# Layers written out, clearing moved to idle GpSimd, loads carried over layer ends, and one block for each stage's addition, norm, turning and first products

## The reference

```python
for l in range(2):                                   # first block
    proj = rms_norm(x, attn_norm[l]) @ w_in[l]       # 1024 x 3328
    mix = three mixers of proj (attention, differential attention, gated scan)
    x = x + mix @ w_out[l]
    hf = rms_norm(x, ffn_norm[l]) @ w_up[l]          # gate and value, 2816 each
    x = x + (gelu(conv(gate)) * value) @ w_down[l]
for l in range(2):                                   # second block
    proj = x @ w_in_2[l]
    mix = rms_norm by head of four mixers of proj    # short conv, MLA, conformer conv, windowed attention
    h = layer_norm(ALPHA * x + mix @ w_out_2[l], ln1_g, ln1_b)
    # 8 heads, each choosing 16 of 16384 experts; computed as a dense product over all of them
    x = layer_norm(ALPHA * h + peer_ffn(h), ln2_g, ln2_b)
```

## Time and profile before

| | |
|---|---|
| runs | 3116.73 us median of 3 (3116.24 to 3126.63) |
| profiled execution | 3117.86 us, of which the span from first to last instruction is 3116.1 |
| busy, share of the span | PE 2696.1 us (87%), VectorE 2165.6 (69%), ScalarE 1465.3 (47%), GpSimd 351.3 (11%) |
| mean granted TensorE clock | 0.909 |
| HBM traffic | 161 GB/s over the span |

### The profile page before, as it was taken

The page is one execution under the profiler, slowest core; times in us unless marked ns, Lnnn a source line. Parts: engine busy times, 40 slices in busy tenths (PEclk is TensorE's granted clock), DMA queues, the critical chain, the costliest instruction groups (busy, mean ns, idle before and its releaser), DMA issues. The chain is left out here.

```text
span 3116.1 us, 57779 instructions
## 1 busy us (share of the span) xinstructions
PE 2696.1 (87%) x16968; PEld 2432.3 (78%) x16968; DVE 2165.6 (69%) x4756; ACT 1465.3 (47%) x2850; POOL 351.3 (11%) x308
## 2 busy tenths in 40 slices
PE   7858978768968579989999999675799899999996
PEld 6657967558966479979997888564799799978885
DVE  5766757656756755887777777557558877767775
ACT  5334545335433334546665555332345456655553
POOL 3130003130002003430000000030024300000000
PEclk9858999769988589999999999885899999999998
DMA  5104545014534045655556777440456555567774
GB/s 189 58 34 142 184 137 181 27 54 154 183 139 138 9 143 178 228 169 175 175 171 230 240 242 240 144 171 1 142 174 229 172 174 173 172 228 239 241 243 146
DMA packets 193620, 504.00 MB, mean 162 GB/s; under 512 B 22496, under 2 KB 88288, under 8 KB 191968
## 3 DMA queue, kind: packets, MB, share of 16 engines
q1 hardware_dynamic: 193504, 502.62, 48.2%
HBM read 467.93 MB, written 34.60 MB: 161 GB/s over the span
## 5 line engine op out<-in xcount | busy, mean ns | idle before, releaser
L165 DVE TENSOR_TENSOR w_lo<-w_raw,w_hi 128x512 fp32r<-128x512 f32 x1376 | 938.5, 686 | 337.1 <-ACT w_hi L156 307.3
L156 ACT ACTIVATE w_hi<-w_raw 128x512 fp32r<-128x512 f32 (+1 forms) x1592 | 925.0, 621 | 301.6 <-PE ffn_up L198 95.9
L196 PE MATMUL up_up<-hT_hi,w_hi 128*128 128x256 f32 x2048 | 596.2, 291 | 26.6 <-DVE w_lo L165 20.5
L197 PE MATMUL up_up<-hT_lo,w_hi 128*128 128x256 f32 x2048 | 582.2, 284 | 0.0
L198 PE MATMUL up_up<-hT_hi,w_lo 128*128 128x256 f32 x2048 | 582.1, 284 | 0.0
L174 POOL TENSOR_TENSOR w_lo<-w_raw,w_hi 128x512 fp32r<-128x512 f32 (+2 forms) x216 | 292.7, 1355 | 1999.4 <-DVE w_lo L165 1981.5
L196 PEld LDWEIGHTS up_up<-hT_hi,w_hi 128*128 128x128 f32 x2048 | 395.3, 193 | 31.0 <-DVE w_lo L165 23.8
L208 PE MATMUL peer_acc<-w_hi,expert_hi 128*128 128x512 f32 x1024 | 400.1, 391 | 7.8 <-DVE w_lo L165 7.8
L209 PE MATMUL peer_acc<-w_lo,expert_hi 128*128 128x512 f32 x1024 | 399.4, 390 | 0.0
L210 PE MATMUL peer_acc<-w_hi,expert_lo 128*128 128x512 f32 x1024 | 399.3, 390 | 0.0
L197 PEld LDWEIGHTS up_up<-hT_lo,w_hi 128*128 128x128 f32 x2048 | 395.9, 193 | 0.0
(11 more groups left out here) (367 smaller groups left out, 4579.8 us busy)
## 6 DMA issues: line engine op xcount, KB each, us to landing
w_raw<-in_peer_u_c SPq DMA_DIRECT2D x256, 512.0 KB, 3.3
w_raw<-in_peer_v SPq DMA_DIRECT2D x256, 512.0 KB, 3.3
w_raw<-in_w_up_c SPq DMA_DIRECT2D x88, 512.0 KB, 3.3
expert_gelu_held<-expert_gelu SPq DMA_DIRECT2D x256, 128.0 KB, 1.7
expert_back<-expert_gelu_held SPq DMA_DIRECT2D x256, 128.0 KB, 3.0
w_raw<-in_w_down SPq DMA_DIRECT2D x44, 512.0 KB, 3.8
w_raw<-in_w_in_r SPq DMA_DIRECT2D x40, 512.0 KB, 3.4
w_raw<-in_w_in_c SPq DMA_DIRECT2D x32, 512.0 KB, 4.4
```

What stands on the lines that cost most here:

```text
L156: self.nc.scalar.activation(self.w_hi[:, k % SLOTS, 0:width], self.raw_half(k, width), ACT.Copy).then_inc(self.sem("w_hi_done"), 1)
L165: self.nc.vector.tensor_tensor(self.w_lo[:, k % SLOTS, 0:width], self.raw_half(k, width), self.w_hi[:, k % SLOTS, 0:width].bitcast(F32), A ...
L196: self.nc.tensor.matmul(bank, hi, self.hT_hi[:, c, :], start=(c == 0), stop=False)
L197: self.nc.tensor.matmul(bank, hi, self.hT_lo[:, c, :], start=False, stop=False)
```

## The change

- The two loops over layers are written out in Python, with constants for l. `new_scope` makes new semaphores for each part of a layer; the old ones are cleared by `sweep` on GpSimd, within the block of the next feed-forward loop or of `up_with_gates`. The weight stream's own semaphores and counters run on through the program.
- The last stage of a layer (`gated_loop`, `DownPhase`) loads the first four pieces of the next one (`after`). Columns of all layers and the rotary table are loaded and made in the first block.
- `transpose_split`, `rms_rows` and, for `ln1` and the first `ln2`, `layer_norm` become entries (`TurnEntry`, `RmsEntry`, `LayerNormEntry`), whose steps stand at the head of the lists of `project` or `gated_loop`, in the same block as the first products, and with them the addition, which reads PSUM. PSUM is held as two sets of four banks, left and right, from stage to stage. The products of a chunk wait for that pair of chunks alone. The norm's factor isn't applied to the rows but to the identity (`diag`), and the turning is a real product with it. The first four halves (`EARLY`) are split inside the entry, all `w_lo` on VectorE. For a layer norm, x itself is finished by `rows`, one of four passes after each weight half from the ninth.
- `head_norm` and `layer_norm` take eps and the mean in ScalarE's Sqrt (scale and bias) and drop one VectorE operation; the mixers' gain of the second kind goes into the copies that evict the turned chunks.
- The last layer norm and the store are `finish`: by token halves, rows loaded in free weight slots beside the last products; GpSimd clears what is left during the store.

```diff
+    def new_scope(self):
+        self.stale += list(self.sems.values())
+        self.sems = {}
+    def sweep(self, pool):
+        for s in self.stale:
+            pool.sem_clear(s)
+            self.nc.release_semaphore(s)
+        self.stale = []
...
+            if entry is not None:
+                entry.chunk_ready(pe, c)
...
+    def chunk_ready(self, pe, c):
+        if c % 2 == 0:
+            pe.wait_ge(self.lo_done, c // 2 + 1)
+    def tensor(self, pe):
+        for t in range(TT):
+            if self.add is not None:
+                pe.wait_ge(self.added, t + 1)
             for c in range(DC):
-                for t in range(TT):
-                    ins = nc.tensor.transpose(ps[:, c, t * P:(t + 1) * P],
-                                              src[:, t, c * P:(c + 1) * P], K.ident[:])
-                ins.then_inc(turned, 1)
-
-        @block.scalar
-        def _(act):
+                ins = self.K.nc.tensor.transpose(self.ps[:, c, t * P:(t + 1) * P], self.src[:, t, c * P:(c + 1) * P],
+                                                 self.K.ident[:])
+                if t == TT - 1 and c % 2 == 1:
+                    ins.then_inc(self.turned, 1)
+    def scalar(self, act):
+        for h in range(EARLY):
+            self.K.split_hi(act, self.k0 + h)
+        self.evict_hi(act)
+    def evict_hi(self, act):
+        A, hi = self.K.nc.scalar, self.K.hT_hi
+        for j in range(DC // 2):
+            act.wait_ge(self.turned, j + 1)
+            if self.gain is None:
+                ins = A.activation(hi[:, 2 * j:2 * j + 2, :], self.ps[:, 2 * j:2 * j + 2, :], ACT.Copy)
+            else:
+                for c in (2 * j, 2 * j + 1):
+                    ins = A.activation(hi[:, c, :], self.ps[:, c, :], ACT.Copy, scale=self.gain[:, c:c + 1])
+            ins.then_inc(self.hi_done, 1)
...
+    def vector(self, dve):
+        for t in range(TT):
+            if self.add is not None:
+                x = self.src[:, t].rearrange("p (h n) -> p h n", h=2)
+                self.K.nc.vector.tensor_tensor(x, x, self.add[:, t], ALU.add).then_inc(self.added, 1)
+        for h in range(EARLY):
+            self.K.split_lo(dve, self.k0 + h)
+        self.evict_lo(dve)
...
+class RmsEntry(TurnEntry):
...
+    def tensor(self, pe):
+        for t in range(TT):
+            pe.wait_ge(self.scaled, t + 1)
             for c in range(DC):
-                act.wait_ge(turned, c + 1)
-                g = 1.0 if gain is None else gain[:, c:c + 1]
-                nc.scalar.activation(K.hT_hi[:, c, :], ps[:, c, 0:SEQ], ACT.Copy,
-                                     scale=g).then_inc(hi_done, 1)
-
-        @block.vector
-        def _(dve):
+                ins = self.K.nc.tensor.matmul(self.ps[:, c, t * P:(t + 1) * P], self.src[:, t, c * P:(c + 1) * P],
+                                              self.diag[:, t, :], start=True, stop=True)
+                if t == TT - 1 and c % 2 == 1:
+                    ins.then_inc(self.turned, 1)
+    def scalar(self, act):
+        A = self.K.nc.scalar
+        for h in range(2):
+            self.K.split_hi(act, self.k0 + h)
+        for t in range(TT):
+            if self.add is not None:
+                act.wait_ge(self.added, t + 1)
+            A.activation(self.junk[:, t, :], self.src[:, t, :], ACT.Square,
+                         accum_out=self.ss[:, t, 0:1]).then_inc(self.squared, 1)
+            act.wait_ge(self.squared, t + 1)
+            A.activation(self.ss[:, t, 1:2], self.ss[:, t, 0:1], ACT.Sqrt, scale=1.0 / D,
+                         bias=self.K.eps[:, 0:1]).then_inc(self.root, 1)
+        for h in range(2, EARLY):
+            self.K.split_hi(act, self.k0 + h)
+        self.evict_hi(act)
+    def vector(self, dve):
+        K, V = self.K, self.K.nc.vector
+        for t in range(TT):
+            if self.add is not None:
+                x = self.src[:, t].rearrange("p (h n) -> p h n", h=2)
+                V.tensor_tensor(x, x, self.add[:, t], ALU.add).then_inc(self.added, 1)
+        for t in range(TT):
+            dve.wait_ge(self.root, t + 1)
+            K.dve.link(dve, V.reciprocal(self.ss[:, t, 2:3], self.ss[:, t, 1:2]))
+            V.tensor_scalar(self.diag[:, t, :], K.ident[:], self.ss[:, t, 2:3], None, ALU.mult).then_inc(self.scaled, 1)
+            for h in (2 * t, 2 * t + 1):
+                K.split_lo(dve, self.k0 + h)
+        self.evict_lo(dve)
...
+class LayerNormEntry(TurnEntry):
...
+    def scalar(self, act):
+        A = self.K.nc.scalar
+        for h in range(2):
+            self.K.split_hi(act, self.k0 + h)
+        for t in range(TT):
+            act.wait_ge(self.mean_done, t + 1)
+            A.activation(self.mv[:, t, 2:3], self.mv[:, t, 1:2], ACT.Sqrt, bias=self.K.eps[:, 1:2]).then_inc(self.root, 1)
+            A.activation(self.centred[:, t, :], self.src[:, t, :], ACT.Identity,
+                         bias=self.minus[:, t:t + 1]).then_inc(self.centre_done, 1)
+        for h in range(2, EARLY):
+            self.K.split_hi(act, self.k0 + h)
+        for j in range(DC // 2):
+            if j % 2 == 0:
+                act.wait_ge(self.turned, j + 1)
+                for c in (2 * j, 2 * j + 1):
+                    A.activation(self.h[:, c, :], self.ps[:, c, :], ACT.Identity, scale=self.gain[:, c:c + 1],
+                                 bias=self.bias[:, c:c + 1]).then_inc(self.shifted[0], 1)
+            act.wait_ge(self.shifted[j % 2], 2 * (j // 2 + 1))
+            A.activation(self.K.hT_hi[:, 2 * j:2 * j + 2, :], self.h[:, 2 * j:2 * j + 2, :],
+                         ACT.Copy).then_inc(self.hi_done, 1)
+    def vector(self, dve):
+        K, V = self.K, self.K.nc.vector
+        link = lambda ins: K.dve.link(dve, ins)
+        for t in range(TT):
+            x = self.src[:, t].rearrange("p (h n) -> p h n", h=2)
+            link(V.scalar_tensor_tensor(x, x, ALPHA, self.add[:, t], ALU.mult, ALU.add))
+            for j in range(2):
+                ins = V.bn_stats(self.stats[:, t, j, :], self.src[:, t, j * 512:(j + 1) * 512])
+            link(ins)
+            link(V.bn_aggr(self.mv[:, t, 0:2], self.stats[:, t].rearrange("p n s -> p (n s)")))
+            V.tensor_scalar(self.minus[:, t:t + 1], self.mv[:, t, 0:1], -1.0, None, ALU.mult).then_inc(self.mean_done, 1)
+            dve.wait_ge(self.root, t + 1)
+            link(V.reciprocal(self.mv[:, t, 3:4], self.mv[:, t, 2:3]))
+            V.tensor_scalar(self.diag[:, t, :], K.ident[:], self.mv[:, t, 3:4], None, ALU.mult).then_inc(self.scaled, 1)
+        for h in range(EARLY):
+            K.split_lo(dve, self.k0 + h)
+        def shift(j):
+            dve.wait_ge(self.turned, j + 1)
+            for c in (2 * j, 2 * j + 1):
+                V.tensor_scalar(self.h[:, c, :], self.ps[:, c, :], self.gain[:, c:c + 1], self.bias[:, c:c + 1],
+                                ALU.mult, ALU.add).then_inc(self.shifted[1], 1)
+        def low(j):
+            dve.wait_ge(self.hi_done, j + 1)
+            two = slice(2 * j, 2 * j + 2)
+            V.tensor_tensor(K.hT_lo[:, two, :], self.h[:, two, :], K.hT_hi[:, two, :].bitcast(F32),
+                            ALU.subtract).then_inc(self.lo_done, 1)
+        for j in range(0, DC // 2, 2):
+            shift(j + 1)
+            low(j)
+            low(j + 1)
...
+    def rows(self, dve, gain, bias):
+        K, V, x = self.K, self.K.nc.vector, self.src
+        dve.wait_ge(self.centre_done, TT)
...
             for q, (src, width) in enumerate(pieces + list(after)):
                 if q >= K.ahead:
                     K.load_piece(sp, k0 // 2 + q, src, width)
...
+            entry.vector(dve)
+            steps = iter(()) if rest is None else rest(dve)
...
+                if k >= 2 * EARLY:
+                    next(steps, None)
...
+            entry.tensor(pe)
...
+            for q, (src, width) in enumerate(after):
+                K.load_piece(sp, at(LAST) // 2 + 1 + q, src, width)
+        @block.gpsimd
+        def _(pool):
+            K.sweep(pool)
...
+                for t in range(TT):
+                    sp.wait_ge(ready, t + 1)
+                    sp.dma_start(out[:, t, :], x[:, t, :]).then_inc(stored, 16)
...
+                dve.wait_ge(*rows_in)
+                for t in range(TT):
+                    dve.wait_ge(root, t + 1)
+                    link(V.reciprocal(mv[:, t, 3:4], mv[:, t, 2:3]))
+                    dve.wait_ge(centre_done, t + 1)
+                    link(V.scalar_tensor_tensor(x[:, t], centred[:, t], mv[:, t, 3:4], gain, ALU.mult, ALU.mult))
+                    V.tensor_tensor(x[:, t], x[:, t], bias, ALU.add).then_inc(ready, 1)
...
+        for l in range(L):
+            first_layer(K, l, K.cols1[:, l], in1[l + 1] if l + 1 < L else in2[0])
+        for l in range(L):
+            second_layer(K, l, K.cols2[:, l], table, in2[l + 1] if l + 1 < L else [])
```

More of the change, by code:

```diff
@@ L785, in _ @@
         def _(act):
[L786 to L787 removed]
+            h0 = 0
```

(15 more changed lines are left out.)

725 lines of the change are left out of this document (383 added, 342 removed).

## The result

The changed kernel takes 2991.03 us (median of 4, 2980.37 to 2992.17), the kernel before in the same comparison 3116.78 (3116.24 to 3126.63): a ratio of 0.9577, with a 95% interval of 0.9552 to 0.9601. The forecast was 2991.0.

A forecast was written before the change was run, and what follows sets the result against it. The prediction took idle chains of short dependent steps between PE's long stretches as the bound; its terms summed to -127.7 us from the profiled 3117.9, giving 2990, forecast as 2991 with some hops costing more, range 2968 to 3028.

The forecast's parts named there:

- Idle chains, not engines, were the gain: Between PE's long stretches: chains of short dependent steps leave PE idle; idle before turnings falls from 174 to some 95 us.
- The price of a turning by a real product ... so the same.: Entry turnings: a float32 product at full clock, 0.115 us, priced like a transposition at half clock, 0.228 each.
- Two table loads: Feed-forward to layer end, ScalarE: one table load before Square, another before the root, 1.28 us each.
- further drain: Table switches on ScalarE: a further 1.38 us each by the Trainium skill, 5.5 us for four; left out of the forecast.
- The clock, 8 us between 0 and 25: First products in twelve places: half clock costs some 25 us; 8 us less was taken, bounds 0 and 25.
- every first product: Kernel before, twelve places: every first product runs at 1.2 GHz, for stretches taken as 3 to 5.5 us.
- Clearing and loads over the ends: Layer ends: clearing moves into loops and weight pieces load before the boundary; inside savings of 14.9, 21.0 and 26.9 us.
- the row passes: Behind the layer norms, three places: passes moved behind the ninth weight half cost 0, without cover up to 4.8 us each.
- Serialised entries: Rival: merged blocks serialise on VectorE and ScalarE, each of twelve entries takes 5 us more, 3051 us; chance 0.12.
- slower by fetched code: Rival: fetching written-out layers' code stalls engines at block ends, some 90 blocks losing 1.6 us each, past 3133; chance 0.03.
- no effect: Rival: something outside the chains, such as weight pieces' landing, holds the first products; 3102 to 3133 us; chance 0.03.
- The clock stays up: Rival: all entries keep 2.4 GHz, 17 us more come back, 2974 us; chance 0.10.

The follow-up runs named there:

- experiment 2: Changed kernel with the twelve entries (addition, norm, turning, evictions) in a block of their own, ended before the products' block: 3040.33 us, ratio 0.9759.
- experiment 3: Changed kernel with GpSimd's clearing taken out of the loops into a block of its own behind each of the first three layers: 3005.81 us, ratio 0.9653.
- experiment 7: Changed kernel with a layer's first four weight pieces loaded at its first block's start instead of in the loop before: 3005.2 us, ratio 0.9619.
- experiment 1: Changed kernel with the seven turnings by real product replaced by transpositions, norm's factor left out of the result: 3005.68 us, ratio 0.9625.
- experiment 6: Changed kernel with transpositions in the seven turnings, norm's factor left out, each transposition issued twice: 2989.64 us, ratio 0.9571.
- experiment 9: Changed kernel without the four passes that write the layer norm's values back to x, in three places: 2986.33 us, ratio 0.9563.
- experiment 5: The changed kernel itself run again, nothing changed, on a second chip: 2994.67, 2985.45, 2980.54, 2992.2 and 2982.65 us.
- experiment 12: Version with earlier start, filling before turnings and early table load, plus filling products in the first layers' first attention: 2983.71 us, ratio 0.9556.
- experiment 10: Changed kernel with 12 or 16 filling float32 products ahead of six of the seven turnings by a real product: 2986.23 us, ratio 0.958.

## Why the prediction was right, and where it was not

- *Idle chains, not engines, were the gain.* Right: gaps 112.7 of 127.0 us, forecast 118.1. The busy time of PE didn't change, and the expert stretches are as long as before within 3 us, most of that directly behind their first products. Of the 127, the merged block is worth 46 to 55, the clearing 23 and the loads 8 (experiments 2, 3 and 7). The rest, shorter chains by token halves, the moved rotary table and the store by halves, was not undone piece by piece.
- *"The price of a turning by a real product ... so the same."* This step failed. I divided the 7.38 us of the earlier trace rows by its 64 records; they are 32 products, each issued as two passes. A real product costs 0.23 at full clock, a transposition half of that (3.65 / 16 at half clock, so 0.114 at full). It made the turning 5.4 to 6.6 us instead of some 3.7 (experiment 1: 1.7 to 2.2 us in each RMS place), and with it the start and the two feed-forward entries late.
- *Two table loads.* Also wrong: the load in front of Square is gone, though ScalarE comes from Gelu and Copy as before; why isn't shown. That 1.28 us happened to pay for most of the turning there. No further drain: Sqrt follows the load by 0.02 us (454.39 + 1.28, then 455.69), so leaving that term out was right.
- *The clock, 8 us between 0 and 25.* Mis-sized. The first 6 us behind eleven first products ran at 0.50 to 0.76 before; now nine of them run at 1.00, one at 0.90 and one at 0.72. (The twelfth is the start's, where the clock has no rows yet.) In sum these stretches stood at 0.50 for 52.1 us before and for 4.7 now, and half of the difference is 24 us: the price of 25 for the whole was right, the third of it that I took was not. Not "every first product" was at half clock, though: at 475.94 and 712.17 the clock fell only 1.1 and 0.4 us later. The stretches other than the two that hold the first kind's mixers are 20.5 us shorter, mostly by it. Experiments 1 and 6 tell why it stayed up behind the turnings by real products: not because they are products, but because they keep PE busy for longer, directly ahead of the first product. The doubled cost of the turning thus bought the clock, and the cheaper turning is no faster in sum. That isn't the whole: 8.6 of the 20.5 us stand behind the four turnings ahead of the out products, which are 16 transpositions as before. In a block of their own (experiment 2) these four stretches lose 5.3 of them again, so there it is in good part that the first product follows at once.
- *What I had no term for:* the first layer's attention at half clock, up to 13.4 us. It isn't a fixed cost of the change: the changed kernel falls on either side of it. The kernel before has scatter of the same size (3113.7 to 3126.7 on one chip); in its one profile both layers kept the full clock there, so where its scatter comes from isn't shown. In the changed kernel's profile it offset the clock's surplus elsewhere. That the forecast met the median to 0.1 us is therefore luck; a sum of these terms is good to some 10 us.
- *Clearing and loads over the ends.* Priced inside the layer-end terms, and right: clearing 6 us at each end (experiment 3), loads 2 to 4 (experiment 7). GpSimd's clearing inside the loops (experiment 3) and the row passes (experiment 9) cost nothing.
- *The rivals.* Serialised entries, slower by fetched code, and no effect are out. "The clock stays up" was largely true behind the entries, but 2974 was missed: the first layer's attention took 9.4 us back, and the gaps, by the turning's price above all, gave 5.4 less than forecast.

**Open.** Why the clock falls at that attention in some executions and not in others. It is not the code ahead of it (experiments 3 and 5 have the same and reach the first scores 82.3 us behind the first product; it fell in one profile and not in the other), a shift of 1.4 us did not take it away (one profile), and filling inside the attention does not prevent it (experiment 12). Nor is it even between the layers: in the twelve profiles of versions with one block, the changed kernel's among them, the clock fell 1.2 to 2.5 us behind the first scores in nine first layers, but in two second layers only (experiments 1 and 7). The head turning just ahead, where PE is busy 1.62 of 3 us (105 to 108), is a candidate; it was not tried. Its code is the same in both layers, so by itself it can't be all.

## What to carry to other kernels

Find the gaps between an engine's long stretches and list, for each, the chain of dependent steps: here blocks ended, semaphores were cleared and weights not yet loaded, and each could be undone by itself (46 to 55, 23 and 8 us). Count instructions, not records, before dividing a row's time. And when a stage's end gets shorter, look at the granted clock behind it: a busier approach can be worth more than a shorter one, and filling an idle approach (experiment 10) gives both.

## What the runs showed of the hardware

- A 128x128 float32 product is two records and twice a transposition's time: 0.23 us at full clock (7.38 / 32; 16 of them in 3.84) against 0.11 (16 transpositions in 3.65 at half clock).
- After 3.6 to 5.2 us without products the granted clock fell to 0.50, between 2.4 us ahead of the turning's start and 1.1 us behind it. With products or doubled transpositions (the changed kernel and experiment 6) it was at 0.50 for 2.8 to 6.1 us of the turning and back at 1.00 before the first product behind it; with 16 transpositions alone (experiment 1) it stayed at 0.50 through the turning and for 2.9 to 5.1 us more. That is no sharp rule: ahead of the out products, after 6.0 or 16.4 us of idling, 16 transpositions alone were followed by 0 to 2.2 us at 0.50 (versions with one block and no filling in every attention), and by 2.9 to 6.2 us in the kernel before, where the first product came 2.6 us behind them.
- A stretch can stay at 0.50 for 31 us while PE is busy 29.5 of them (108 to 139), and the same work run at 1.00 with PE busy 15.8 of 17.8.
- Clearing one layer's semaphores on GpSimd in a block of its own takes some 6 us.
